# Expert routing in a two-block transformer kernel: the index lookup of a token half in three long vector operations instead of thirty-two short ones

## The reference, cut to what matters

```python
def peer_ffn(h, w_q, sub_keys, u, v):        # 8 heads, 128 keys, top 16, 16384 experts
    q = (xc @ w_q).reshape(-1, PEER_HEADS, 2, half)
    s = jnp.einsum('thpd,pkd->thpk', q, sub_keys).astype(jnp.float32)
    sv, si = lax.top_k(s, PEER_TOPK)
    cand = (sv[:, :, 0, :, None] + sv[:, :, 1, None, :]).reshape(-1, PEER_HEADS, PEER_TOPK * PEER_TOPK)
    cand_id = (si[:, :, 0, :, None] * PEER_NKEYS + si[:, :, 1, None, :]).reshape(...)
    cv, ci = lax.top_k(cand, PEER_TOPK)
    eid = jnp.take_along_axis(cand_id, ci, axis=-1)
    g = jax.nn.softmax(cv, axis=-1)
    ue = u[eid]
    ve = v[eid]
    a = jax.nn.gelu(jnp.einsum('td,thkd->thk', xc, ue)).astype(jnp.float32)
    return jnp.einsum('thk,thkd->td', (g * a).astype(ve.dtype), ve)
```

## Time and profile before

| | |
|---|---|
| median of 3 runs | 3108.29 us (3108.18 to 3108.99) |
| the profiled execution | 3113.82 us, of which the span is 3112.0 us |
| PE busy | 3070.1 us, 99% of the span |
| DVE busy | 2243.8 us, 72% |
| ACT busy | 1638.4 us, 53% |
| POOL busy | 711.2 us, 23% |
| mean granted PE clock | 0.996 of full speed |

### The profile page before, as it was taken

The page is one execution under the profiler, slowest core; times in us unless marked ns, Lnnn a source line. Parts: engine busy times, 40 slices in busy tenths (PEclk is TensorE's granted clock), DMA queues, the critical chain, the costliest instruction groups (busy, mean ns, idle before and its releaser), DMA issues.

```text
span 3112.0 us, 58454 instructions
## 1 busy us (share of the span) xinstructions
PE 3070.1 (99%) x19936; PEld 2735.9 (88%) x19936; DVE 2243.8 (72%) x4133; ACT 1638.4 (53%) x3088; POOL 711.2 (23%) x710
## 2 busy tenths in 40 slices
PE   7999999999999999999999999999999999999999
PEld 6789999988888876899999877779988999988897
DVE  6649978877777436698888777777757777765654
ACT  2125578864444344355888544455456545445643
POOL 0108745520000110286455100000101010011000
PEclk9999999999999999999999999999999999999999
DMA  8745555568887441455444778777865687784454
GB/s 307 244 133 179 183 162 168 168 208 272 267 265 242 139 129 42 133 185 176 142 135 135 245 260 266 260 251 270 257 225 175 237 266 267 277 272 145 152 183 149
DMA packets 178355, 635.34 MB, mean 204 GB/s; under 512 B 24074, under 2 KB 24082, under 8 KB 177843
## 3 DMA queue, kind: packets, MB, share of 16 engines
q1 hardware_dynamic: 134562, 490.96, 47.6%
q0 software_dynamic: 43648, 142.77, 13.6%
q10 hardware_dynamic: 16, 0.01, 0.0%
HBM read 630.36 MB, written 9.53 MB: 206 GB/s over the span
## 4 chain that ended last, share of the span: by engine, by line
PE 87%; DVE 7%; DMA 3%; ACT 1%; DVEq 1%; issue 1%; POOL 0%; SPq 0%; ACTq 0%
PE ps L828 21%; PE ps L626 12%; PE ps L628 12%; PE ps L627 11%; PE ps L612 7%; PE ps L810 6%; PE ps L662 2%; PE ps L1272 2%; PE ps L1271 2%; DMA ring<-stream 1%; PE ps L1113 1%; PE ps L1040 1%; PE ps L940 1%; PE ps L696 1%; PE ps L756 1%
## 5 line engine op out<-in xcount | busy, mean ns | idle before, releaser
L1932 DVE TENSOR_TENSOR unit_low<-ring,unit_high 128x1024 fp32r<-128x1024 f32 x480 | 638.6, 1330 | 159.2 <-ACT unit_high L1406 150.6
L1406 ACT CAST unit_high<-ring 128x1024 fp32r<-128x1024 f32 x524 | 548.1, 1046 | 226.4 <-PE ps L628 167.2
L628 PE MATMUL ps<-expert_x_high,unit_low 128*128 128x256 f32 x1952 | 552.7, 283 | 0.0
L626 PE MATMUL ps<-expert_x_high,unit_high 128*128 128x256 f32 x1536 | 443.4, 289 | 2.3 <-DVE unit_low L1932 1.8
L627 PE MATMUL ps<-expert_x_low,unit_high 128*128 128x256 f32 x1536 | 429.5, 280 | 0.0
L628 PEld LDWEIGHTS ps<-expert_x_high,unit_low 128*128 128x128 f32 x1952 | 367.7, 188 | 0.0
L828 PE MATMUL ps<-unit_low,expert_high 128*128 128x512 f32 x1012 | 323.5, 401 | 2.9 <-DVE unit_low L1932 2.9
L828 PE MATMUL ps<-unit_high,expert_low 128*128 128x512 f32 x1012 | 318.1, 395 | 0.0
L828 PE MATMUL ps<-unit_high,expert_high 128*128 128x512 f32 x1012 | 315.7, 393 | 0.4 <-ACT unit_high L1406 0.3
L626 PEld LDWEIGHTS ps<-expert_x_high,unit_high 128*128 128x128 f32 x1536 | 291.4, 190 | 7.1 <-issue 2.6
L1831 ACT CAST expert_high<-arena 128x256 fp32r (+1 forms) x256 | 103.7, 406 | 356.9 <-PE ps L828 356.9
(11 more groups left out here) (399 smaller groups left out, 7052.5 us busy)
## 6 DMA issues: line engine op xcount, KB each, us to landing
ring<-stream SPq DMA_DIRECT2D x754, 512.0 KB, 3.9
arena<-stream SPq DMA_DIRECT2D x160, 512.0 KB, 4.4
score<-ada POOLq DMA_DIRECT2D x128, 512.0 KB, 5.1
arena<-ada POOLq DMA_DIRECT2D x96, 512.0 KB, 5.3
arena<-bias_tiles POOLq DMA_DIRECT2D x48, 192.0 KB, 2.7
arena<-ada SPq DMA_DIRECT2D x8, 1024.0 KB, 14.3
bias_tiles<-bias_rows POOLq DMA_DIRECT2D x8, 768.0 KB, 15.0
arena<-gate_home POOLq DMA_DIRECT2D x7, 512.0 KB, 9.9
```

The lines of the kernel that those rows point to most:

```text
L626: pe.matmul(out, hi[:, kt, :], xh[:, kt, :], start=(kt == 0), stop=False)
L628: mm = pe.matmul(out, lo[:, kt, :], xh[:, kt, :], start=False, stop=(kt == KD - 1))
L1406: nc.scalar.copy(hi, raw_of(unit)).then_inc(whi_ready, 1)
L1932: V.tensor_tensor(out=lo, in0=raw_of(unit), in1=hi, op=ALU.subtract).then_inc(wlo_ready, 1)
```

## The change

A token half's lookup becomes, for each w, one comparison of 2048 columns, one multiplication of 2048 and one sum of 2048 columns to 128, each followed by a call of `step`. The intermediate lies in the candidates' place in `score`, not in `r_outT`. A half now has 6 calls of `step` in the lookup instead of 16, so `PLAIN_STEPS` goes from 72 to 62. The exp of the second half follows unit 44 instead of 45.

```diff
-PLAIN_STEPS = 72
-EXP_AFTER = (13, 45)
+PLAIN_STEPS = 62
+EXP_AFTER = (13, 44)
...
-        eq = r_outT[:].rearrange("p w t -> p (w t)")[:, 0:2 * TOPK * TOPK].rearrange("p (n c) -> p n c", c=TOPK)
...
+                    eq = sc.rearrange("p g n -> p (g n)").rearrange("p (k c) -> p k c", c=TOPK)
+                    eq4 = sc.rearrange("p g n -> p (g n)").rearrange("p (h k c) -> p h k c", h=PH, c=TOPK)
                     for w in range(2):
-                        for c in range(0, PH, 2):
-                            k0 = c * TOPK
-                            V.tensor_tensor(out=eq, in0=r_abf[:, w, k0:k0 + 2 * TOPK].unsqueeze(2).to_broadcast([P, 2 * TOPK, TOPK]),
-                                            in1=iota[:, 0:TOPK].unsqueeze(1).to_broadcast([P, 2 * TOPK, TOPK]), op=ALU.is_equal)
-                            dve.drain()
-                            step()
-                            for h in range(2):
-                                part = eq[:, h * TOPK:(h + 1) * TOPK, :]
-                                V.tensor_tensor(out=part, in0=part,
-                                                in1=si4[:, c + h, w, :].unsqueeze(1).to_broadcast([P, TOPK, TOPK]), op=ALU.mult)
-                            dve.drain()
-                            V.tensor_reduce(r_out[:, tt, w, k0:k0 + 2 * TOPK], eq, AX.X, ALU.add)
-                            dve.drain()
-                            step()
+                        V.tensor_tensor(out=eq, in0=r_abf[:, w, :].unsqueeze(2).to_broadcast([P, NE, TOPK]),
+                                        in1=iota[:, 0:TOPK].unsqueeze(1).to_broadcast([P, NE, TOPK]), op=ALU.is_equal)
+                        dve.drain()
+                        step()
+                        V.tensor_tensor(out=eq4, in0=eq4, in1=si4[:, :, w, :].unsqueeze(2).to_broadcast([P, PH, TOPK, TOPK]),
+                                        op=ALU.mult)
+                        dve.drain()
+                        step()
+                        V.tensor_reduce(r_out[:, tt, w, :], eq, AX.X, ALU.add)
+                        dve.drain()
+                        step()
```

## The result

The changed kernel took 3124.03 us (median of 5 executions, 3120.87 to 3129.0), against 3108.29 us (5 executions, 3107.04 to 3112.58) for the kernel before: a ratio of 1.0047 [1.0034, 1.006]. (The ratios and their 95% intervals are taken over all executions, so they can differ a little from the quotient of the two medians, 1.0051 here.) It is slower by about half a per cent. The forecast was 3120 us within 3103 to 3130, and slower.

A forecast was written before the change was run, and what follows sets the result against it. The prediction took PE, busy 3070 of 3112 us, to bound the kernel. Costs of 18.9 us less gains of 6.7 gave net +12.2 on the 3108.3 us median: 3120 us, range 3103 to 3130.

The forecast's parts named there:

- the cover of 1.6 us: How far POOL's lows were taken to be ahead of PE, read at unit 34: about 1.6 us.
- Part 1: First half's lookup: DVE's 2048-column two-input operations shut out POOL's lows and PE waits; cost 5.5 us a layer.
- The walk: Step-by-step timing of DVE, POOL and PE over units 12 to 17, first layer; PE ends unit 17 at 284.8.
- Part 2: Second half's w = 0 comparison and multiplication, reached sooner, shut out POOL's lows up to 47; cost 2.0 us a layer.
- Part 3: Lows 48 to 52: a 2.3 us DVE operation between each two makes PE wait; cost 1.95 us a layer.
- Part 4: Waits that vanish: units 57 to 58 gain 3.7 us (first layer) and 2.2 (second); units 46 and 47 gain 0.4, twice.
- rival 3: Slower still: PE's 1.8 us waits bring the granted clock down, +3 to +10, 3123 to 3130 us; chance 0.18.
- Rival 1: Faster: lows further ahead than 1.6 us, so long operations don't make PE wait; 3105.5 or 3101.6 us; chance 0.17.
- Rival 2: A draw: locks cost about half, meeting POOL's rests or highs piled up ahead; 3113 us; chance 0.2.

The follow-up runs named there:

- compare_twice: The changed kernel with each comparison of the first half done twice: 3127.64 us, ratio 1.0056 to the kernel before.
- first_half_only: The kernel before with the long lookup in the first token half alone, exp still behind unit 45, PLAIN_STEPS 62: 3124.57 us, ratio 1.0035.
- psum_operands: The changed kernel with one of the two inputs of each comparison and multiplication in PSUM, same columns and order: 3110.70 us, ratio 1.0 to the kernel before.
- second_half_only: The kernel before with the long lookup in the second half alone, PLAIN_STEPS 71, exp behind unit 45: 3112.65 us, ratio 1.0006.
- lows_last: The changed kernel with PLAIN_STEPS 67 instead of 62, so DVE's own lows begin behind the whole lookup: 3125.09 us, ratio 1.0052 to the kernel before.
- exp_45: The changed kernel with the exp of the second half back behind unit 45: 3119.38 us, ratio 1.003 to the kernel before.
- psum_rests: The changed kernel with one lookup input in PSUM and PLAIN_STEPS 67, DVE's lows behind the whole lookup: 3104.92 us, ratio 0.998 to the kernel before.

## Why the prediction was right, and where its sizes were off

**What bounds the kernel, and the cover of 1.6 us: right.** PE's busy time moved by 2.1 us only, and the first lock of the first half already made PE wait (unit 12 took 3.60 us for 2.84, where I had put 0.8 us of waiting). compare_twice shows the same from the other side: with the cover used up, each further lock costs PE 1.7 us.

**Part 1, 5.5 us a layer: the mechanism right, the size too large; 4.54 / 4.36 measured.** This is the term that was mis-sized, for two reasons. The walk had PE wait 0.8, 1.75, 1.75 and 1.8 us. By the gelus above and those between them it waited 0.76 for unit 12 and 1.55 for unit 13, 1.06 for units 14 and 15 together, and 1.55 for unit 16: 4.9 us, not 6.1. First, the order. In the walk the comparison of w = 1 follows the sum at once and shuts out low 14; in the trace POOL's low at 269.45 went first, so that unit 14 had its low in time. The prediction named this order and priced it at 5.4 to 5.9, but that was reckoned wrongly: with 2.2 us a lock the same walk ends unit 17 at 284.4, which is 5.1. Second, the lock. I took 2.2 us for each time that POOL was shut out, from 512-column operations in a row; the 2048-column ones held it 2.0 to 2.06 us, and a unit under a lock took 4.39 us, not 4.6. That takes off the remaining 0.6 to 0.7. first_half_only shows the term alone (5.01 / 4.53), psum_operands shows it gone.

**Part 2, 2.0 us a layer: right, 2.29 / 2.35.** Its reason too: it is the sooner end of the first half that brings DVE to this place while POOL is at its lows. second_half_only leaves the first half alone, and there at most POOL's last low is met. Some luck is in the size: units 35 and 36 took 3.71 and 4.40 us in the first layer, waits of 0.9 and 1.55, where I had 0.2 and 1.8, so POOL's lead was smaller and the lock shorter than I took them for.

**Part 3, 1.95 us a layer: right, 1.91 / 2.03,** and without any lock, as psum_operands (same cost, no lock) and lows_last (cost gone) show.

**Part 4, gains of 3.7 and 2.2, and 0.4 twice: direction right, size small; 4.07 and 2.64, and 0.44 / 0.24.** 57 to 58 came to 3.49 us and not 3.9, because six transposes without a wait took less than I had from three:

```profile
404.25 0.82 PE L1285 MATMUL ps<-prm,r_out 128*128 128x128 f32 x6
404.82 0.37 PE L625 MATMUL ps<-expert_x_high,unit_high 128*128 128x256 f32 x1
```

They took 0.82 us where I had doubled 0.55, and the next product began 0.57 us behind their start. The 0.4 between 43 and 47 is there and comes mostly of the exponential's place: in exp_45, where DVE is in time too, only 0.10 / 0.05 of it is left. But the same move makes 1.0 us a layer of part 3's cost; my walk for part 3 had the exponential in its new place, so the sum held it, but I had not seen that it was this edit's doing.

**The sum.** 12.2 us net were forecast; from stage to stage the two profiles show 10.1. Of the 2.1 between, 18.9 - 17.5 = 1.4 come of the costs and 7.4 - 6.7 = 0.7 of the gains. The medians differ by more, 3124.03 - 3108.29 = 15.7 us (ratio 1.0034 to 1.006, or 10.6 to 18.6 us). Part of that is in the choice of the profiled execution: that of before, at 3113.82 us, was 5.5 above its median and held the clock fall behind unit 58, some 1.6 us by the working of rival 3, which another execution may not have. The other kernels point the same way: for each of the eight the timed difference to before is 1 to 6 us above the one that its stretch from 8 to 58 gives. What lies outside these two stretches varies from 2810.7 to 2816.8 us over the ten traces, and before's 2816.6 is among the longest. Beyond the 1.6 us the cause stays open, as only one execution of before has a trace. So that 3120 lies within 4 us of 3124 is in part luck: with every term at its traced size the same sum would have given 3118.

**The rivals.** Rival 1 (the lows far enough ahead) fell with the first wait, that for unit 12. Rival 2 (half the price) had a part in it: POOL's locks cost 13.5 us and not 15, so a tenth and not a half. Rival 3 (the clock falls behind the waits) did not happen. The stretch of the first layer with the most waits (us, then busy us of PE, PEld, DVE, ACT and POOL, granted clock, DMA share, GB/s):

```profile
262.00:272.00 10.00, 8.23 (x67) 7.82 (x66) 9.78 (x4) 4.01 (x6) 10.00 (x4) 1.00 0.46 157
272.00:282.00 10.00, 7.91 (x65) 7.51 (x64) 9.78 (x9) 6.93 (x10) 10.00 (x3) 1.00 0.47 152
```

PE stood still for 1.77 and 2.09 us of each 10, DVE and POOL were hardly ever idle, and the granted clock was 1.00. It was 1.00 in the other stretches with such waits, too.

## What to carry to other kernels

Before widening a DVE operation, ask who shares its way to SBUF and by how much that engine's results are ahead: here a longer operation saved DVE 67 us off the path and cost PE a wait each time that it shut POOL out for longer than the lead of 1.6 us. If both inputs are in SBUF and POOL has two-input work on the path, move a small, repeated operand to PSUM; that alone took the changed kernel from 3124 to 3111 us. In this case the long operations were worth nothing even then: short ones with the same operands were as fast. After each edit read every stretch again: a stall that leaves one can stand in the next, as with lows_last.

## What the runs showed of the hardware

- A two-input DVE operation of 2048 columns takes 2.29 us with no POOL work at its side, and up to 4.32 us behind a low of POOL's. With one input in PSUM it takes 2.29 us beside a low, and the low 2.41.
- Not only two-input operations wait. A copy of 8 columns took 0.16 us in one place of the changed kernel and 2.37 in another, where it ended with a low of POOL's (the pair from 255.13 to 259.88). With the operands in PSUM such rows stay: 2.38 us in psum_rests.

```profile
257.53 2.37 DVE L2586 COPY small<-pick 128x8 f32<-128x8 f32 x1
...
328.12 0.16 DVE L2586 COPY small<-pick 128x8 f32<-128x8 f32 x1
```

- The length of the waits around the transposes doesn't tell whether the granted clock falls. Behind 1.41 and 0.68 us (before, first layer) it fell, to a mean of 0.68 in the 3 us at 396 and of 0.51 in the 3 us at 397, close to the lower of its two levels, 1.2 GHz; behind 1.50 and 0.68 (before, second layer) it stayed at 1.00. In first_half_only it stayed at 1.00 behind 1.34 and 0.68 and fell to 0.70 behind 1.53 and 0.68. Waits of up to 1.3 us on lows, several in 20 us, left it at 1.00. What decides is not settled.
